# Two layers on one core: a weight chunk loaded earlier, the last gate computed in two halves, one extra unread product

## The reference, cut to what matters

```python
for l in range(2):
    mod = silu(c) @ w_mod[l] + b_mod[l]
    sh1, sc1, g1, sh2, sc2, g2 = split(mod, 6)
    h = rms_norm(x, norm_mix[l]) * (1 + sc1) + sh1
    y = four_mixers(h @ w_in[l]) @ w_out[l]
    x = x + g1 * y
    h = rms_norm(x, norm_ffn[l]) * (1 + sc2) + sh2
    f = swiglu(h) if l == 0 else moe(h)     # 8 experts, the 2 best of each token
    x = x + g2 * f
return rms_norm(x, norm_final)
```

## Time and profile before

| | |
|---|---|
| median of 3 runs | 1573.01 us (1572.98 to 1574.33) |
| profiled execution, its own time | 1574.65 us |
| its span, from first to last instruction | 1572.9 us |
| PE busy | 98% of the span |
| DVE busy | 83% |
| ACT busy | 62% |
| DMA, mean over the span | 306 GB/s |
| mean granted clock of PE | 0.993 |

### The profile page before, as it was taken

The page is one execution under the profiler, slowest core; times in us unless marked ns, Lnnn a source line. Parts: engine busy times, 40 slices in busy tenths (PEclk is TensorE's granted clock), DMA queues, the critical chain, the costliest instruction groups (busy, mean ns, idle before and its releaser), DMA issues.

```text
span 1572.9 us, 19303 instructions
## 1 busy us (share of the span) xinstructions
PE 1544.6 (98%) x7851; PEld 1255.5 (80%) x7851; DVE 1310.8 (83%) x1186; ACT 972.1 (62%) x852; POOL 49.9 (3%) x118
## 2 busy tenths in 40 slices
PE   7999999999999989999999999999999999999997
PEld 3886789999888568888888888888888888888885
DVE  5888888888674479989799899889998989999987
ACT  2532434444444357777777777777777787777775
POOL 5300100000000010000000000000000000000000
PEclk9999999999999999999999999999999999999999
DMA  9765888887823169999999999999999999999990
GB/s 349 267 236 193 282 315 324 306 296 268 307 84 131 54 230 363 371 364 350 330 370 345 365 367 360 335 356 354 358 370 371 342 333 370 349 368 372 344 353 30
DMA packets 158182, 481.04 MB, mean 306 GB/s; under 512 B 4234, under 2 KB 8502, under 8 KB 158086
## 3 DMA queue, kind: packets, MB, share of 16 engines
q1 hardware_dynamic: 156160, 475.02, 82.1%
q0 software_dynamic: 1392, 3.58, 0.7%
q10 hardware_dynamic: 534, 1.13, 0.2%
HBM read 478.66 MB, written 1.05 MB: 305 GB/s over the span
## 4 chain that ended last, share of the span: by engine, by line
PE 95%; DVE 2%; DMA 2%; ACT 1%; issue 0%; SPq 0%; DVEq 0%; ACTq 0%
PE bank L1175 20%; PE bank L1176 20%; PE bank L1177 20%; PE bank L868 6%; PE bank L1053 4%; PE bank L1092 3%; PE bank L1094 3%; PE bank L1093 3%; PE bank L865 3%; PE bank L1068 2%; PE bank L1069 2%; DMA ring<-in_w_mod_dram 2%; PE bank L1070 2%; PE bank L1206 2%; PE bank L1146 1%; PE bank L784 1%
## 5 line engine op out<-in xcount | busy, mean ns | idle before, releaser
L1836 DVE TENSOR_TENSOR ring_low<-ring,w_high 128x2048 fp32r<-128x2048 f32 x336 | 768.5, 2293 | 101.3 <-ACT w_high L2267 94.1
L2267 ACT ACTIVATE w_high<-ring 128x2048 fp32r<-128x2048 f32 x336 | 646.2, 1925 | 238.9 <-PE bank L1177 229.7
L1175 PE MATMUL bank<-w_high,x_high 128*128 128x512 f32 x896 | 355.8, 397 | 0.6 <-issue 0.6
L1176 PE MATMUL bank<-ring_low,x_high 128*128 128x512 f32 x896 | 355.5, 397 | 0.0
L1177 PE MATMUL bank<-w_high,x_low 128*128 128x512 f32 x896 | 352.7, 394 | 0.0
L1175 PEld LDWEIGHTS bank<-w_high,x_high 128*128 128x128 f32 x896 | 168.6, 188 | 41.7 <-DVE ring_low L1836 1.7
L1177 PEld LDWEIGHTS bank<-w_high,x_low 128*128 128x128 f32 x896 | 168.2, 188 | 39.1
L1176 PEld LDWEIGHTS bank<-ring_low,x_high 128*128 128x128 f32 x896 | 168.3, 188 | 37.0
L2206 ACT ACTIVATE tmp_r<-ring 128x1024 fp32r<-128x1024 f32 x84 | 89.2, 1064 | 148.0 <-PE bank L1094 86.5
L1175 PE MATMUL bank<-w_high,act_high 128*128 128x512 f32 x448 | 177.5, 396 | 0.3 <-DVE ring_low L1836 0.3
L1176 PE MATMUL bank<-ring_low,act_high 128*128 128x512 f32 x448 | 175.8, 392 | 0.0
(11 more groups left out here) (353 smaller groups left out, 1690.4 us busy)
## 6 DMA issues: line engine op xcount, KB each, us to landing
ring<-in_moe_w_dram SPq DMA_DIRECT2D x168, 2048.0 KB, 7.9
ring<-in_w_mod_dram SPq DMA_DIRECT2D x23, 2048.0 KB, 10.8
ring<-in_ffn_w_dram SPq DMA_DIRECT2D x21, 2048.0 KB, 14.0
ring<-in_w_in_dram SPq DMA_DIRECT2D x7, 2048.0 KB, 18.7
ring<-in_w_out_dram SPq DMA_DIRECT2D x4, 2048.0 KB, 13.4
ring<-in_w_in_dram SPq DMA_DIRECT2D x4, 1024.0 KB, 14.8
ring<-in_w_mod_dram SPq DMA_DIRECT2D x2, 1024.0 KB, 16.0
gate_row<-in_b_mod_dram POOLq DMA_DIRECT2D x4, 512.0 KB, 7.6
```

The costliest lines, as they stand in the source:

```text
L1175: mm(out_, x_h, w_h, start=first, stop=False)
L1176: mm(out_, x_h, w_l, start=False, stop=False)
L1836: tt_(moe_low(u, m // 2)[:, c], moe_slot(u, m // 2)[:, c], w_high[:, m % HIGHS, :].bitcast(F32), ALU.subtract).then_inc(low_made, 1)
L2267: act(w_high[:, m % HIGHS, :], moe_slot(u, m // 2)[:, c], ACT.Copy).then_inc(high_made, 1)
```

## The change

Three edits. In `chunks` the first half of `g1` moves ahead of the two w_out halves (it becomes number 13, the w_out halves become 14 and 15). The last gate (`g2` of layer 1) is no longer computed in one piece at the end of `routing`: its first half is computed between `norm_x(3)` and `norm_h(3)`, its second between the first fill of `x_slots` and the first `x_low`. One more unread block of 512 columns is issued behind the last product of `routing`.

```diff
@@ chunks
         mod_chunk(0, "sc2", 1)
+        mod_chunk(0, "g1", 0)
         wout_chunks(0)
-        mod_chunks(0, "g1")
+        mod_chunk(0, "g1", 1)
@@ PE, routing
                 mark(ins.then_inc(route_t.sem, 1), route_t, "most")
+                keep_clock(bank[7], steady, 1)
@@ DVE
-            def gate(l, which, b):
+            def gate(l, which, b, halves=(0, 1)):
 
                 rep = 2 * l + which
                 eng.wait_ge(s_gate, 16 * (rep + 1))
                 eng.wait_ge(gate_t.sem, gate_t.at("sum", rep))
-                for half in range(2):
+                for half in halves:
@@ DVE, routing
                 done_(nc.vector.memset(chosen[:, :, NE:, :], 0.0).then_inc(route_v.sem, 1), "idle")
-                gate(1, 1, (bank[0], bank[1]))
@@ DVE, experts
+                    if q == 0 and part == 0:
+                        gate(1, 1, (bank[0], bank[1]), (1,))
                     fill_low(part, pair(q, 0), 0)
@@ DVE, the layer loop
                 norm_x(2 * l + 1)
+                if l:
+                    gate(1, 1, (bank[0], bank[1]), (0,))
                 norm_h(2 * l + 1)
```

## The result

| | before | changed |
|---|---|---|
| median of the runs | 1573.71 us (20 runs) | 1578.16 us (20 runs) |
| profiled execution, its own time | 1574.65 us | 1580.4 us |
| its span | 1572.9 us | 1578.6 us |

The ratio of the runs is 1.0023, with a 95% interval of 1.0014 to 1.0033. That is 3.6 us more (1573.71 x 0.0023), between 2.2 and 5.2. The two medians differ by 4.45 us, which lies in the same interval.

A forecast was written before the change was run, and what follows sets the result against it. PE was taken to run without a pause from the first expert (572.69 us) to the end, so delays before it carry through. Chunk order -0.7, norm +5.4, routing's end -1.0 gave +3.7 on 1573.0: 1576.7 us, range 1573.9 to 1579.0.

The forecast's parts named there:

- The stall: Last norm: DVE stands still 5.3 us for the bias load before the first gate half, PE waiting too; step +5.4 us.
- The gate half in the norm: Last norm: first gate half waits for its bias, delaying `h_t` by 4.95 us; +5.4 us with slower router products, bounds +4.65 to +5.8.
- The gate halves out of the routing's end: Routing's end: DVE fills `x_slots` after half the gather, without two gate halves ahead; -1.0 us, bounds -0.5 and -1.3.
- The unread block as a help to the gather's clock: Before the last `dispatch`: costs nothing and may keep the gather at full clock; its worth is inside the -1.0 us.
- The chunk order: FFN: one load less queued, so the first `sh1` half lands in 8.0 us, not 8.58; -0.7 us, bounds 0 and -0.8.
- the FFN pause stops costing clock: Rival, 198 to 206 us: shorter pause leaves the clock at 2.4 GHz, -1.65 us; 1569.9 us at the edge; chance 0.03.
- The stall without the slower clock: Rival: router products keep full clock or the FFN's half-clock stretch goes; step +4.7, sum +2.0 to +3.0 us; chance 0.30.
- The bias is there in time: Rival, last norm: bias lands by 553.4 us, the half costs 0.71 us, sum -1.0 us, 1572.0 us; chance 0.08.
- W_out comes late: Rival, FFN: w_out lands at 133.2 us, PE stops 2.4 us at 130.8; +6 to +8 us, 1579 to 1581; chance 0.05.

The follow-up runs named there:

- e2: The kernel before with the gate split alone, without the new chunk order and the unread block: 1579.24 us, ratio 1.0032 to the kernel before.
- e5: The changed kernel with the first gate half's bias loaded early into another, free buffer: 1572.22 us, ratio 0.9990 to the kernel before.
- e9: The changed kernel with the 512 KB final norm row loaded by POOL ahead of the bias: 1580.17 us, ratio 1.0036 to the kernel before.
- e8: The changed kernel without the unread block: 1578.11 us, ratio 1.0022 to the kernel before.
- e7: The changed kernel with the bias loaded in two 256 KB halves, the first gate half waiting for its own: 1576.11 us, ratio 1.0017 to the kernel before.
- e12: The kernel before, unchanged, run once more for its trace alone: 1573.5 us in one run.
- e3: The kernel before with the unread block alone: 1574.14 us, ratio 0.9997 to the kernel before.
- e6: The changed kernel with the first gate half moved from the norm into DVE's wait for token positions: 1572.43 us, ratio 0.9996 to the kernel before.
- e11: The kernel before, unchanged, timed against itself as control: 1573.78 us, ratio 0.9996.
- e1: The kernel before with the new chunk order alone: 1573.67 us, ratio 0.9986 to the kernel before.
- e10: The kernel before with the new chunk order alone, a second time: 1574.04 us, ratio 0.9995 to the kernel before.

## Why the prediction was right, and where its parts were not

Forecast +3.7 us, measured +3.6 by the ratio and +4.45 by the medians. The stall, the large term, has the size, the place and the slower clock that the prediction gave, and the gates' gain at the gather has its size. That the sum comes out to 0.1 us is luck: the measurement leaves 2.2 to 5.2, the traces add up to 3.1, two of the smaller reasons did not hold, and a gain of 0.8 us was not in the sum.

**The gate half in the norm, +5.4: right.** DVE's idle time was forecast at 5.3 us and is 5.34, `h_t` at +4.95 and is +4.93, `logits_t` at +5.4 and is +5.42. The router products were to lose 1.0 to 1.7 us if half clock fell on them. Twelve took 4.10 us where full clock gives 2.7, so 1.4 more. In all five traces with the stall this happened, behind a wait of PE of 4.02 to 7.11 us (4.10, 4.18, 4.19 and 4.30 us, and 5.29 in e2). e2, e5 and e9 bind the loss to this wait: the gate edits alone make it, its removal ends it, a longer one enlarges it.

The figure of the Trainium skill, "DMA: Bandwidth & Descriptors", section "Anatomy of one DMA", 2.0 us plus the bytes over 436 GB/s, was weighed in the prediction against the earlier trace rows. The runs bear the rows out: 7.2 us, 7.3 in e8, and about as long for half the bytes in e7. The only bias load that comes near the figure is e5's on idle queues, 3.3 us for 256 KB, for which the figure gives an estimate of 2.6 us.

**The gate halves out of the routing's end, -1.0: right at the gather, and one gain was missing.** From `logits_t` to the first expert the changed kernel gained 1.94 us (5.42 - 3.48). 1.14 of it are what the term spoke of (from the gather's first product to the fill 2.26 us in place of 3.40), inside its bounds of 0.5 to 1.3. The other 0.81 us come from a step that the prediction did not have, in the routing's small operations. Before, the first comparison took 0.99 us; e12's trace shows it in the same way (in order of time, DVE):

```profile
556.12 2.60 DVE L1836 TENSOR_TENSOR ring_low<-ring,w_high 128x2048 fp32r<-128x2048 f32 x1
...
559.97 0.99 DVE L1766 TENSOR_TENSOR route<-route,route_c 128x16 f32<-128x16 f32 x1
```

POOL beside it:

```profile
557.17 3.76 POOL L763 TENSOR_TENSOR h_high<-xn,xn_high 128x1024 fp32r<-128x1024 f32 x1 [0.60 <-ACT xn_high L2099]
```

and POOL in the changed kernel:

```profile
559.93 2.34 POOL L764 TENSOR_TENSOR h_high<-xn,xn_high 128x1024 fp32r<-128x1024 f32 x1 [0.60 <-ACT xn_high L2104]
```

with DVE's comparison long behind it:

```profile
568.16 0.17 DVE L1768 TENSOR_TENSOR route<-route,route_c 128x16 f32<-128x16 f32 x1
```

POOL's second subtraction starts in e12 while DVE's weight rest runs and takes 3.76 us instead of 2.34; it ends at 560.93 us, and DVE's comparison, begun at 559.97, ends at 560.96. Where the stall has pushed DVE's work behind POOL's (all five such traces), each takes its short time: 2.34, 2.29 and 0.17 us, within 0.01. In the eight traces without the stall these are 3.77, 2.60 and 0.99 us or within 0.01 of it. The Trainium skill, "SBUF — State Buffer", section "Who interferes with whom", says that a DVE instruction with two SBUF inputs and a GpSimd instruction that reads SBUF contend for ports that are an exclusive lock, and that issue order decides who blocks. The traces agree, in both directions. In e12 the rest is over at 558.72, and 2.34 us behind that is 561.06, where POOL's operation in fact ends at 560.93; the comparison then waits for it. So the stall gave back 0.8 us, as a side effect of pushing DVE's work behind POOL's. (The weight rest's own 0.31 us, which the prediction allowed for, was not on the path, since `logits_t` waited for PE.)

**The unread block as a help to the gather's clock: not borne out.** It costs nothing, as forecast (e3, e8). But it does not decide the gather's clock. In the stalled kernels the half-clock stretch fell on the router products, and in four of five the gather's first half was then at full clock, with the block or without (e8). Without the stall the stretch came at the gather in both kernels with the gate halves moved (e5, e6), with the block, and in five of the six with the gates at their old place; only e3 is without it there. So the -1.14 us are there only with the stall that costs 5.4; where the stall is taken away, the edit is worth 0 (first expert 22.47 in e5 and 22.71 in e6, against 22.13 to 22.55 in the kernels with the gates at their old place). Whether a gather at full clock would make it worth about a microsecond in a kernel without the stall no run shows.

**The chunk order, -0.7: about half, and by another way.** The step said that the first `sh1` half would land in 8.0 us instead of 8.58. It does in the trace after (7.99), but in the old order e11 and e12 have 8.01 and 8.03: the 8.58 were that one run's. What the order removes is the wait of DVE for the first `g2` half. From the first FFN product to DVE's first step on the `sh1` half it is 25.52, 25.81, 25.95, 26.09 and 25.35 us in the old order, mean 25.74, and 25.05 to 25.43 in the new, mean 25.28 over eight traces, so -0.46. The whole column "FFN" says -0.4 as well: 375.39 in the mean of e2, e11 and e12, 375.02 in the eight of the new order. What half clock behind the pause would give back was taken as 0, "since most of the pause is left", and 0 is right for another reason: it costs nothing there. The changed trace has no such stretch behind the pause and gains nothing by it: from DVE's first step on the `sh1` half to the last residual addition it is 349.73 us in the changed kernel, and 349.73 or 349.74 in e1, e5 and e11, which have the stretch. So the condition of the rival "the FFN pause stops costing clock" came true, and its 1.65 us did not. DVE's pace, not PE's, fits this; no run tests it by itself.

**The sum by the traces** is -0.4 for the order and +3.5 at the first expert (+5.42 - 1.94), 3.1 us, inside the measured interval of 2.2 to 5.2. At the first expert the forecast was +4.4 us (5.4 - 1.0), and it is +3.48. Against the forecast the order is 0.3 us short, the gather's gain 0.1 us larger, and the routing's 0.8 us were not in it. It is carried to the end as forecast: from the first expert product to the last instruction it is 1000.41 us, before 1000.25, and in all thirteen traces 999.7 to 1000.5.

**The rivals.** "The stall without the slower clock" would have shown router products of 2.7 us; none of five traces has them. "The bias is there in time" is what e5 builds: that rival gave -1.0 us, and the measured ratio (0.9973 to 1.0007) can't tell this from nothing. By the trace it is the order's -0.4 and nothing at the first expert; the part that is missing is the gather's. "W_out comes late": no wait of PE there in any trace.

**A version better than both** did not come out. e5 (change with an early bias) and e10 (order alone) measure 0.9990 and 0.9995 with intervals that reach over 1; the control e11 gave 0.9996.

## What to carry to other kernels

Before an instruction that waits for a transfer is moved forward, read the issue and the landing of that transfer, not its old wait: the old place may hide a landing of 7 us completely. Count what stands behind it on its engine, and what the engine that is fed by it does after standing still. A small load takes longer beside a full queue: here 256 KB took 3.3 us alone and 6.6 beside SP's loads, so move the issue to a place where the queues are idle, and the instruction may follow. And take a stretch at half clock for a thing that one trace has and the next has not: of three traces of the unchanged kernel one had a stretch near 516 us worth 1.7 us, and a single pair of traces would have given it to the edit.

## What was not expected of the hardware

- The 512 KB bias load from POOL took 7.2 us from issue to landing in the changed kernel, and 9.46 us with one more such load ahead of it (e9). Two loads of 256 KB had the first one there after 7.3 us (e7). Some 4.0 us of it pass before the first packet; 256 KB with nothing else on the queues had its first packet after 1.24 us and was there after 3.3 (e5). Until POOL's first packet SP's queue moved 389 GB/s (1.50 MB in 3.86 us), 97.9% of the engines' time.
- DVE's subtraction of 128x2048 (2.60 us instead of 2.29) and POOL's of 128x1024 (3.77 instead of 2.34) hold each other up when they meet, and POOL's holds up a DVE comparison of 16 columns (0.99 instead of 0.17). Copies and reductions of DVE that ran beside the same POOL operation kept their 0.17 us.
- Where half clock falls is not the kernel's alone. The same kernel before has 377.35, 375.82 and 375.08 us in the column "FFN"; the first holds the stretch near 516 us, and the other two differ by DVE's waits for transfers. The control's twelve runs lie between 1569.1 and 1578.7 us.
- Half clock does not always cost time. Behind the pause in the FFN it made no difference (349.73 or 349.74 us with it and without it); near 516 us it cost 1.7 us, and on the router products 1.4.
